# Sixteen V rows of each half gathered behind the next half's U rows, and the first modulation in two halves

## What is computed

```python
mod = silu(cvec) @ w_mod + b_mod
sh_a, sc_a, g_a, sh_f, sc_f, g_f = split(mod, 6)
h = rmsnorm(x, norm_attn) * (1.0 + sc_a) + sh_a
# h @ w_in feeds differential attention and a gated DeltaNet
x = x + g_a * (concatenate([o_da, o_dn]) @ w_out)
h = rmsnorm(x, norm_ffn) * (1.0 + sc_f) + sh_f
x = x + g_f * peer(h)

def peer(h):
    q = (h @ w_pq).reshape(T, 8, 2, 128)
    s = einsum('thpd,hpnd->thpn', q, sub_keys)
    sv, si = top_k(s, 16)                  # 16 of 128 keys, twice per head
    top_s, pos = top_k(all 256 sums of pairs, 16)
    eidx = the 128 experts of a token, out of 16384
    coef = softmax(top_s) * gelu(h . expert_u[eidx])
    return sum over the 128 of coef * expert_v[eidx]
```

## Time and profile before

| | us |
|---|---|
| median of 3 runs | 1592.37 |
| the runs | 1590.33, 1592.37, 1596.22 |
| the profiled execution, its own time | 1579.69 |
| its span | 1577.7 |
| PE busy | 865.6 (55%) |
| DVE busy | 813.6 (52%) |
| POOL busy | 749.9 (48%) |
| ACT busy | 277.6 (18%) |

### The profile page before, as it was taken

How to read it: one execution, slowest core, us unless ns; L and a number is a source line. 1 busy time by engine, 2 the same in 40 slices (tenths; PEclk the granted TensorE clock), 3 DMA queues, 4 the chain that set the end, 5 groups by cost and what they waited for, 6 DMA issues and landing times.

```text
span 1577.7 us, 14365 instructions
## 1 busy us (share of the span) xinstructions
PE 865.6 (55%) x4990; PEld 500.8 (32%) x4990; DVE 813.6 (52%) x2047; ACT 277.6 (18%) x662; POOL 749.9 (48%) x794
## 2 busy tenths in 40 slices
PE   4999998799567776787620675400442005500254
PEld 2566867556353355543210651000110001100010
DVE  2443234687484277851597146897515760087301
ACT  4234443122241232421000020000100000000000
POOL 0001000453446644456676226676667666676663
PEclk9998999899798999899755887655685557755576
DMA  9234446995659988799999729999999999999996
GB/s 394 91 140 151 161 167 254 375 390 215 240 182 356 343 310 316 241 395 352 364 404 357 297 72 375 359 397 364 354 376 376 402 346 335 359 402 364 347 368 234
DMA packets 120295, 486.09 MB, mean 308 GB/s; under 512 B 13344, under 2 KB 14240, under 8 KB 115616
## 3 DMA queue, kind: packets, MB, share of 16 engines
q0 software_dynamic: 111056, 404.28, 68.4%
q1 hardware_dynamic: 9168, 80.90, 13.2%
HBM read 482.50 MB, written 2.62 MB: 307 GB/s over the span
## 4 chain that ended last, share of the span: by engine, by line
DVE 17%; issue 17%; PE 14%; POOL 13%; DMA 6%; another core or an unknown queue 4%; ACT 1%; POOLq 0%; DVEq 0%; ACTq 0%
PE bank L1357 13%; DVE big L2086 11%; POOL big L988 10%; DMA big<-in_ev,idx 2%; POOL big L977 2%; DMA big<-in_ev,rowT 2%; DMA big<-in_eu,consts 2%; DVE hT L2086 1%; POOL hT L988 1%; PE bank L1363 1%; PE bank L1475 0%; DVE big L1876 0%; DVE dn_tok L1970 0%; DVE sq L2112 0%
## 5 line engine op out<-in xcount | busy, mean ns | idle before, releaser
L2086 DVE CUSTOM_DVE_ANT_0 big<-big,hnow 128x1024 f32<-128x1024 f32 x315 | 377.4, 1218 | 193.2 <-DMA big<-in_eu,consts 127.9
L1357 PE MATMUL bank<-big,W 128*32 128x512 f32 x1296 | 259.7, 835 | 167.6 <-DMA big<-in_ev,idx 64.0
L977 POOL DMA_INDIRECT big<-in_eu,consts x236 | 223.4, 947 | 103.4 <-issue 71.6
L988 POOL DMA_INDIRECT big<-in_ev,rowT x197 | 190.5, 967 | 153.5 <-PE bank L1357 76.6
L1357 PE MATMUL bank<-hT,wring 128*128 128x128 f32 (+1 forms) x896 | 143.3, 319 | 40.4 <-issue 32.2
L1363 PE MATMUL bank<-consts 128*128 128x128 f32 x6 | 2.4, 392 | 294.3 <-DVE consts L2101 294.3
L1357 PEld LDWEIGHTS bank<-big,W 128*32 128x32 f32 x1296 | 53.4, 136 | 332.3 <-issue 319.7
L988 POOL DMA_INDIRECT big<-in_ev,idx x118 | 111.7, 947 | 68.2 <-issue 33.3
L1357 PEld LDWEIGHTS bank<-hT,wring 128*128 128x128 f32 x896 | 120.4, 202 | 64.6 <-issue 41.4
L1357 PE MATMUL bank<-big 128*128 128x128 f32 x720 | 100.1, 288 | 40.6 <-issue 23.0
L977 POOL DMA_INDIRECT big<-in_eu,idx x79 | 75.1, 951 | 99.1 <-DVE coef L2086 57.4
(11 more groups left out here) (294 smaller groups left out, 1379.8 us busy)
## 6 DMA issues: line engine op xcount, KB each, us to landing
wring<-in_wch SPq DMA_DIRECT2D x29, 2048.0 KB, 9.2
big<-in_wch SPq DMA_DIRECT2D x6, 1536.0 KB, 8.8
big<-in_eu,consts POOLq DMA_INDIRECT x236
big<-in_ev,rowT POOLq DMA_INDIRECT x197
tok<-in_wch SPq DMA_DIRECT2D x6, 512.0 KB, 9.9
big<-in_ev,idx POOLq DMA_INDIRECT x118
xs<-in_x SPq DMA_DIRECT2D x1, 1536.0 KB, 6.6
out_y<-xs SPq DMA_DIRECT2D x3, 512.0 KB
```

What stands on the lines that cost most here:

```text
L977: nc.gpsimd.indirect_dma_start(row(slot), None, eu, bass.IndirectOffsetOnAxis(ap=idx[t][:, n:n + 1], axis=0)).then_inc(rows_in[slot], 16)
L988: nc.gpsimd.indirect_dma_start(row(slot), None, ev, bass.IndirectOffsetOnAxis(ap=rowT[t][:, n:n + 1], axis=0)).then_inc(rows_in[slot], 16)
L1357: return nc.tensor.matmul(out, lhsT, rhs, start=first, stop=last)
L2086: V.tensor_tensor_reduce(row(slot), row(slot), hnow[:, :], 1.0, 0.0, ALU.mult, ALU.add, coef[t % 2][:, n:n + 1]).then_inc(dot_ready, 1)
```

## The change

1. `gather_order`: from half (1, 0) on, only the first 48 V rows of a half (batches 0 to 11) are gathered ahead of the next half's 64 U rows; the last 16 (batches 12 to 15) come behind them. The last half keeps its 64 together.
2. The first modulation in halves of four feature blocks: the `mod` chunks are stored in the order of `MOD_PART`, so that chunks 0 and 1 are shift and scale of features 0 to 511; `scales(0)` and `modulate` run by half, on ACT (tile 0) and DVE (tiles 1, 2), and PE's first `channels` waits for each half in turn.
3. Tile 1's second half of scores lies in `ops`, and SP's load of `nout` no longer waits for the expert numbers.
4. `STAGES`: rows 16 to 23 use 5 homes and no longer those in `ops`.
5. New entries in `SCALE` (shown) and `EARLIER` (not shown), which reorder steps.

```diff
@@ -57,6 +57,7 @@
           + [("out", 0, 0), ("out", 1, 0)] + [("pq", i, 0) for i in range(4)] + [("mod", 10, 0), ("mod", 11, 0)]
           + [token_chunk(c, 1) for c in DEFER]
           + [("out", 0, 1), ("out", 1, 1)] + [("pq", i, 1) for i in range(4)])
+MOD_PART = (0, 2, 1, 3) + tuple(range(4, 12))
 CHUNK_NO = {c: n for n, c in enumerate(CHUNKS)}
 STORED = [c for c in CHUNKS if c[2] == 0]
 LEAD = CHUNKS.index(("pq", 0, 0))
@@ -69,14 +70,14 @@
 PAIR_OF = {td: n for n, pair in enumerate(PAIRS) for td in pair}
 
 ROWS = 12
-STAGES = [(16, [8, 9, 10, 11, 20, 21, 22, 23, 24]), (24, [8, 9, 10, 11, 20, 21, 22, 23, 24]), (48, [8, 9, 10, 11, 20]), (152, [8, 9, 10, 11, 12, 13, 14, 15, 16, 17, 18, 19, 20]), (160, [8, 9, 10, 11, 20]), (208, [4, 5, 6, 7, 8, 9, 10, 11, 20]), (768, [0, 1, 2, 3, 4, 5, 6, 7, 8, 9, 10, 11, 20])]
+STAGES = [(16, [8, 9, 10, 11, 20, 21, 22, 23, 24]), (48, [8, 9, 10, 11, 20]), (152, [8, 9, 10, 11, 12, 13, 14, 15, 16, 17, 18, 19, 20]), (160, [8, 9, 10, 11, 20]), (208, [4, 5, 6, 7, 8, 9, 10, 11, 20]), (768, [0, 1, 2, 3, 4, 5, 6, 7, 8, 9, 10, 11, 20])]
 QUADS = 4
 HALF = SLOTS // 2
 QUARTER = HALF // 2
 BATCHES = HALF // QUADS
 FILLS = BATCHES // 4
 HALVES = [(t, a) for t in range(NT) for a in range(2)]
-ALONE = {(0, 0): 64, (0, 1): 64, (1, 0): 64, (1, 1): 64, (2, 0): 64}
+BEHIND = 16
 RING0, RINGN = 4, 4
 
 
@@ -84,15 +85,13 @@
 
 
     out = [("gu", 0, n) for n in range(HALF)]
+    held = []
     for k, (t, a) in enumerate(HALVES):
         mine = [("gv", t, a, b, j) for b in range(BATCHES) for j in range(QUADS)]
         following = [("gu", u, HALF * c + n) for u, c in HALVES[k + 1:k + 2] for n in range(HALF)]
-        first = ALONE.get((t, a), 0)
-        out += mine[:first]
-        for n in range(0, len(mine) - first, QUADS):
-            out += mine[first + n:first + n + QUADS] + following[n:n + QUADS]
-        rest = len(mine) - first
-        out += following[rest:]
+        now = len(mine) - BEHIND if following and k >= 2 else len(mine)
+        out += held + mine[:now] + following
+        held = mine[now:]
     return out
 
 
...
-SCALE = {'dn_scores': 0.8, 'channels': 1.1, 'x_turn': 1.1, 'key_score': 1.0, 'score': 0.8, 'dn_decay': 0.8, 'dn_p': 1.0, 'top_key': 0.9, 'gu': 1.1, 'chosen': 1.1}
+SCALE = {'dn_scores': 0.8, 'channels': 1.1, 'x_turn': 1.1, 'key_score': 1.0, 'score': 1.0, 'dn_decay': 0.8, 'dn_p': 1.0, 'top_key': 0.9, 'gu': 1.1, 'chosen': 1.1, 'v_batch': 1.0, 'mod': 1.0}
...
@@ -338,11 +337,12 @@
         add(("mod", m), ("PE", 0, 2.6, ("mod", m), 1), ("ACT", 0.65),
             after=[("load", "mod", m, 0), ("mod_turn", m - 1) if m else None])
         add(("mod_turn", m), ("PE", 0, 0.9, ("mod_turn", m), 1), ("DVE", 0.25), after=[("mod", m)])
-    for w in range(2):
-        add(("scales", w), ("DVE", 0.3), after=[("mod_turn", (3, 9)[w])])
-    add(("modulate", 0), ("ACT", 0, 3.0, ("modulate",)), after=[("scales", 0), ("x_turn", 0, 0)])
-    add(("modulate", 1), ("DVE", 0, 5.0, ("modulate",)), after=[("scales", 0), ("x_turn", 0, 1), ("x_turn", 0, 2)])
-    mixed = [("modulate", 0), ("modulate", 1)]
+    add(("scales", 1), ("DVE", 0.3), after=[("mod_turn", 9)])
+    for half in range(2):
+        add(("scales", 0, half), ("DVE", 0.3), after=[("mod_turn", 2 * half + 1)])
+        add(("modulate", 0, half), ("ACT", 0, 1.6, ("modulate", half)), after=[("scales", 0, half), ("x_turn", 0, 0)])
+        add(("modulate", 1, half), ("DVE", 0, 2.5, ("modulate", half)), after=[("scales", 0, half), ("x_turn", 0, 1), ("x_turn", 0, 2)])
+    mixed = [("modulate", t, half) for t in range(2) for half in range(2)]
     for b in range(12):
         add(("channels", b), ("PE", 0, 5.3, ("channels", b), 1), ("ACT", 0.95), ("DVE", 3.4),
             after=mixed + [("load", "dn", b // 4, 0), ("silu", b - 3) if b >= 3 else None,
@@ -656,7 +656,7 @@
 
         def sco(t, hh):
 
-            return (xo[:, hh, :], (xo[:, 1, :], ops[:, 3072:4096])[hh], ops[:, 1024 * hh:1024 * hh + 1024])[t]
+            return (xo[:, hh, :], ops[:, 2048 + 1024 * hh:3072 + 1024 * hh], ops[:, 1024 * hh:1024 * hh + 1024])[t]
 
         def pqT(t, n):
...
@@ -877,8 +877,6 @@
                         sp.wait_ge(*product.at("s", (i - 2) % 4, 0))
                     sp.dma_start(subkeys(i, t), subk[i]).then_inc(sk_in[i % 2], 16)
             sp.wait_ge(*squares.at(1, 2))
-            for q in range(2):
-                sp.wait_ge(*ids_ready.at(1, 0, q))
             sp.dma_start(xo[:, 1, :], nout).then_inc(nout_in, 16)
             for t in range(NT):
...
@@ -1050,11 +1048,12 @@
                                                bias=modT[:, 24 * w + k, v:v + 1], scale=scl[:, w, k, v:v + 1])
                 return ins
 
-            def modulate():
-
-                act.wait_ge(*scl_ready.at(0))
-                act.wait_ge(*hT_ready.at(0, 0, 1))
-                by_feature(0, 0, range(KD), hT[:, 0]).then_inc(*modulated.next(0))
+            def modulate(half):
+
+                ks = range(4 * half, 4 * half + 4)
+                act.wait_ge(*scl_ready.at(0, half))
+                act.wait_ge(*hT_ready.at(0, 0, half))
+                by_feature(0, 0, ks, hT[:, 0, 4 * half:4 * half + 4]).then_inc(*modulated0.next(half))
 
             def channels(b):
@@ -1394,14 +1393,14 @@
 
             def channels(c):
 
-                if c == 0:
-                    for t in range(NT):
-                        pe.wait_ge(*modulated.at(t))
                 pe.wait_ge(*chunk_here("dn", c // 4, 0))
                 b = begin("chT", c)
                 w = chunk("dn", c // 4, 0)
                 o = (c % 4) * P
                 for k in range(KD):
+                    if c == 0 and k % 4 == 0:
+                        pe.wait_ge(*modulated0.at(k // 4))
+                        pe.wait_ge(*modulated.at(2, k // 4))
                     ins = mm(b[:, 0:T].rearrange("p (t n) -> p t n", t=NT), w[k][:, o:o + P], hT[:, :, k, :],
                              k == 0, k == KD - 1)
...
                 q = (Q_NA, Q_NF)[w]
-                V.scalar_tensor_tensor(out=scl[:, w, :, :], in0=modT[:, 24 * w + 8:24 * w + 16, :], scalar=1.0,
-                                       in1=col(Q[:, q:q + 8], 2), op0=ALU.add, op1=ALU.mult
-                                       ).then_inc(*scl_ready.next(w))
-
-            def modulate():
-
-                dve.wait_ge(*scl_ready.at(0))
+                a, n = (0, 8) if w else (4 * half, 4)
+                V.scalar_tensor_tensor(out=scl[:, w, a:a + n, :], in0=modT[:, 24 * w + 8 + a:24 * w + 8 + a + n, :], scalar=1.0,
+                                       in1=col(Q[:, q + a:q + a + n], 2), op0=ALU.add, op1=ALU.mult
+                                       ).then_inc(*scl_ready.next(w, half))
+
+            def modulate(half):
+
+                ks = slice(4 * half, 4 * half + 4)
+                dve.wait_ge(*scl_ready.at(0, half))
                 for t in (1, 2):
-                    dve.wait_ge(*hT_ready.at(0, t, 1))
-                    ins = V.tensor_tensor(hT[:, t], hT[:, t], col(scl[:, 0, :, 1], P), ALU.mult)
+                    dve.wait_ge(*hT_ready.at(0, t, half))
+                    ins = V.tensor_tensor(hT[:, t, ks], hT[:, t, ks], col(scl[:, 0, ks, 1], P), ALU.mult)
                 link(ins)
                 for t in (1, 2):
-                    V.tensor_tensor(hT[:, t], hT[:, t], col(modT[:, 0:KD, 1], P), ALU.add
-                                    ).then_inc(*modulated.next(t))
+                    V.tensor_tensor(hT[:, t, ks], hT[:, t, ks], col(modT[:, ks, 1], P), ALU.add
+                                    ).then_inc(*modulated.next(t, half))
 
             def channels(b):
```

More of the change, by code:

```diff
@@ L155, in at @@
         return self.sem, self.counts.at.get((self.name,) + key, 1)
-SCALE = {'dn_scores': 0.8, 'channels': 1.1, 'x_turn': 1.1, 'key_score': 1.0, 'score': 0.8, 'dn_decay': 0.8, 'dn_p': 1.0, 'top_key': 0.9, 'gu': 1.1, 'chosen': 1.1}
-EARLIER = {('experts', 0, 0, 0): 200.0, ('slot_gates', 1, 0): 15.0, ('experts', 1, 0, 0): 50.0, ('experts', 1, 0, 1): 50.0, ('dn_done', 1, 1): 50.0, ('v_batch', 0, 0, 15): 100.0, ('dn_done', 2, 1): 100.0, ('dn_done', 1, 0): 100.0, ('dot', 0, 63): 100.0, ('slot_gates', 2, 0): 100.0, ('coef', 1, 0): 200.0, ('qk_turn', 2): 150.0, ('dn_scores', 1, 0): 200.0, ('value', 2, 3): 100.0, ('dn_p', 1, 1, 3): 75.0, ('o_turn', 2): 100.0, ('da_turn', 2): 15.0, ('query', 3, 1): 200.0, ('expert_rows', 0, 0): 150.0, ('dn_scores', 2, 0): 200.0, ('top_key', 0, 0): 50.0, ('mod', 5): 30.0, ('value', 1, 3): 30.0, ('qk_turn', 1): 100.0, ('coef', 0, 1): 100.0, ('experts', 2, 0, 1): 50.0, ('top_key', 2, 0): 100.0, ('token', 1, 2): 200.0, ('resid', 0, 1): 15.0, ('mod', 9): 15.0, ('experts', 0, 0, 1): 15.0, ('experts', 0, 1, 0): 30.0, ('experts', 2, 1, 1): 100.0, ('dn_vb', 2, 0): 15.0, ('dn_vb', 1, 1): 100.0, ('h_turn', 2): 100.0, ('dn_vb', 2, 1): 75.0, ('dn_done', 2, 0): 50.0, ('expert_rows', 0, 1): 15.0}
@@ new lines @@
```

(18 more changed lines are left out.)

## The result

The changed kernel takes 1599.87 us (median of 12 runs, 1594.46 to 1607.91), the kernel before in the same rounds 1593.16 us (12 runs, 1588.49 to 1600.3). The ratio is 1.0045, 95% interval 1.0028 to 1.0062: 7 us slower. That is under the half per cent that I set as the bound of "no change", but the interval excludes a gain, and even equal times. The measured time lies 3 us above the range of 1571 to 1597.

A forecast was written before the change was run, and what follows sets the result against it. It took TensorE to bound the front and DMA-bound expert gathers the back. −2.2 − 4.7 − 6.3 + 3.9 = −9.3 us, taken from 1592.4, gave 1583.1 us; range 1571 to 1597.

The forecast's parts named there:

- The start: First modulation in halves: PE starts its first projection earlier, −2.2 us, bounds 0 and −3, carried on whole.
- The held rows: POOL's three waits behind a half's last U row shrink by 1.3, 3.7 and 1.3 us; −6.3 in all.
- The choice for tile 2: In V(1,1), PE and POOL wait for tile 2's expert indices; net +3.9 us, bounds −3.7 and +10.
- Rival B: Slower: PE stuck at the second index transpose behind VectorE's whole selection, 18 us there; 1601 us and more; chance 0.13.
- rival D: VectorE's selection for tile 2 blocks the gathers for its length, 16 us; time 1597 us; chance 0.03.
- The middle: From 554 to 671 us, the tables' new order fills idle on VectorE and PE; −4.7 us, bounds −10 and +4.
- "−3.4" for three dots: Three dots moved into VectorE's idle 7.48 us before 563.49, ahead of tile 2's exponentials; −3.4 us.
- "−1.3" on PE: Four transposes and four matmuls on PE leave the middle's busy stretch for idle ones; −1.3 us.
- The homes and the interplay of the parts: Fewer homes for rows 16 to 23, and the score home, put at nothing; the parts' terms simply added.
- "Nothing but fewer bytes would shorten this": U rows of half (1,1), 1008 to 1096 us: 64 gathers in 88.00 us at DMA share 0.99.
- The basis: The profiled execution, 1579.69 us against a median of 1592.37, was supposed to have waits in the same places.

The follow-up runs named there:

- after_expo_early: The changed kernel with expo (2,0) back in front of dots 67 to 69 on VectorE; ratio to the kernel before 1.0025 (1.0000 to 1.0050).
- after_old_tables: The changed kernel with the SCALE and EARLIER tables of before, keeping held rows, halved modulation and homes; ratio to the kernel before 0.9970 (0.9946 to 0.9993).
- mod_only: The kernel before with only the modulation in halves; ratio to the kernel before 0.9978 (0.9954 to 1.0002).

## Why the prediction was wrong, by its steps

- **The start, −2.2 us:** right. PE starts 2.6 us earlier; alone it gave 0.9978, 3.5 us, though with an interval that reaches no change.
- **The held rows, −6.3 us:** right, mechanism and size. The waits are 3.94, 3.61 and 3.87 us (forecast 3.1, 4.0, 3.3), 5.3 us less than before in all, and the gather order alone gives 0.9967, 5 us.
- **The choice for tile 2, +3.9 us:** the wait was right, 6.22 us (forecast 6.6), then 1.59; the time of the whole is 2.6 us in the two comparisons, within their intervals. Rival B, slower by a long wait at the second index transpose, didn't come: these 1.59 us stand for its 18. The selection didn't block the gathers: the longest of V(1,1) in after took 1.44 us in place of 0.95. The Trainium skill (page "SBUF — State Buffer", section "SBUF: two separate sides") speaks of operations of VectorE in a two-port mode. That the selection runs in one I assumed; no run here shows it, so rival D wasn't the page's forecast, as I had it, but mine.
- **The middle, "−3.4" for three dots and "−1.3" on PE:** the step that failed, by sign. In place of −4.7 the tables' new order of the middle costs about 6.5 us, 11 of the 16 us between forecast and result. The dots gave nothing (after_expo_early). I read 7.48 us of idle on VectorE as room, although the same row names no releaser: VectorE waited for scores of PE, and PE and ScalarE had stood themselves, for 3.40 and 4.28 us. And I costed two of the steps that the tables move in the middle and none in V(0,1), where a gate's transposes came ahead of the query on which POOL's wait of 10.64 us hangs. That the bounds were −10 to +4 shows how little the rows supported −4.7; their middle, −3, with the sum at −7.6, would still have been on the wrong side.
- **The homes and the interplay of the parts, put at nothing:** some 4 us are left between the parts alone and after_old_tables. No run tells whether it is the homes, the parts in company or noise.
- **"Nothing but fewer bytes would shorten this"**, of U(1,1) at share 0.99, entered no term of the sum. On the slower chips no kernel shortened it (88.3 to 93.4 us), but the faster ones need 80 us for the same bytes, and in the profile of before too POOL sends 44 gathers of it in a row at its own pace.
- **The basis:** the rows are of one execution 0.8% under the median, under all twelve timed beside the changed kernel, in the very stages where the dispute lay.

What stays open: which step of the tables costs the rest of V(0,1), and whether the halved modulation lengthens the stand. Of the kernels profiled on the slower chips and not paced, four without it have U(0,1) at 129 to 133 us and nine with it at 135 to 143, and PE's longest idle time in its first 50 us is 1.5 to 5.2 us without and 5.9 to 17.4 with it. But only mod_only (135.2 for 130.2 to 132.7) was run beside kernels without it, and a stage of this kind varies by 4 us between two executions. The run that should have told fell on a faster chip. On the slower chips the change without its tables beats both kernels, 0.9970, and with the earlier coefficients 0.9949; the held rows alone do it as well, 0.9967.
